# The second norm of x from three sums gathered in the down product, with the update of x split between VectorE and GpSimd

## The chip, the cores and the metric

The kernel runs on one core of a Trainium2 chip. The core has five engines with queues of their own: TensorE (matmul), VectorE, ScalarE, GpSimd and SyncE (which here only issues DMAs). They meet only through semaphores. The metric is the device time of one execution in microseconds.

## The reference, cut to what matters

Two transformer blocks follow one another on x of 512 positions by 1024 channels, all in float32. The change lies where the first block ends and the second begins:

```
# end of the first block
f = (silu(h @ w_gate) * (h @ w_up)) @ w_down
x = x + rms_norm(f, norm_ffn_post_g)
# start of the second block
h = rms_norm_2(x, norm1_g) * (1 + sc1) + sh1
proj = h @ w_in_2          # the linear attention's and the dilated attention's inputs
# rms_norm(v, g) = v * rsqrt(mean(v * v) + 1e-6) * g, the mean over the 1024 channels
```

The root of the second norm needs the mean square of the new x, which is the old x plus f times its own root and gain. Written out, with r the first root, o = f times gain: sum(x_new^2) = sum(x^2) + 2 r sum(x o) + r^2 sum(o^2).

## The kernel before, in words

Everything is kept transposed: channels on the 128 partitions in 8 tiles, the 512 positions along the row. A weight tile (`raw`, 128x1024, three slots) is loaded by SyncE, rounded by ScalarE to fp32r (`split_hi`, L1079), and VectorE makes the rest `w_lo` (`split_lo`, L1549). A product is three fp32r matmuls for each of 8 channel tiles (hi x hi, hi x lo, lo x hi, L598), so a unit of one output tile has 24.

*Down* (`down`, L864 on TensorE, L1358 on ScalarE, L1906 on VectorE) makes the 8 tiles of f. Each takes three weight slots in the order 1, 0, 2, and lands in O0 or O1 by turns. When a tile is done, ScalarE squares it into `sq` (L1305) and copies it into `oT` (L1306), and VectorE adds the square to `sqacc` (L1565) and computes two pieces of the second block's modulation vector from `ada` (L1883). Behind the last tile TensorE sums over the partitions with a matrix of ones, in plain f32: first `sqacc` (L612), then the square of the last tile (L614), both into S0.

*The first root and the update.* ScalarE makes the root with a logarithm and an exponential (`inverse_rms`, L1090 and L1091). VectorE (`post_norm`, L1587) then goes through the 8 tiles of x: `hbuf` = oT x gain x root (L1598), x = x + hbuf (L1606). ScalarE squares each new tile (L1083) and TensorE adds it to S0 (`sum_squares_by_tile`, L616). Behind its eight tiles VectorE splits the weights in slot 2 and clears `gacc` (L1943), which raises `m2_free`.

*The second root and h.* `inverse_rms` again; then, tile by tile, VectorE multiplies x with the root (L1579), ScalarE scales and shifts (L1097) and rounds to `h_hi` (L1098), VectorE takes the remainder `h_lo` (L1574). TensorE takes up each tile as it comes, for two units at once (`two_units`, L633): one gives the gate input `glr`, the other the first query tile.

*What follows.* ScalarE copies `glr` (L1389), splits slot 1 and goes on in a fixed order. TensorE multiplies `glr` with `wgate` (L893), then runs units with the level products of the linear attention (L923) between them. VectorE makes cumulative sums and seven masks before it raises the signal for the first level products.

The order on every engine is that of the code; nothing is scheduled at run time. Three queues matter here. SyncE waits for `m2_free` before it loads `wgate`, and all later weight tiles stand behind that in its queue. GpSimd issues the loads of `ada` and then waits for `m2_free` too, to number rows and columns for the masks. `h_hi` and `oT` are the same memory.

Of the kernel before, what the change touches and what calls it, by code (L numbers as in the profile page):

```python
# [26 lines left out]
P = 128  # L27
S = 512
# [150 lines left out]
def build(nc, a, out):  # L179
    with ExitStack() as ctx:  # L180
# [57 lines left out]
        (oT,), _ = region(h_at, ("oT", [KD, S], F32))  # L238
# [120 lines left out]
        x_sq_r = signal("x_sq_r")  # L359
        f_f32 = signal("f_f32", credit=1)  # L360
# [81 lines left out]
        def _(pool):  # L442
# [138 lines left out]
        def _(pe):  # L581
# [33 lines left out]

            def sum_squares_by_tile():  # L616

                for k in range(KD):
                    pe.wait_ge(sq_g[k % 2], w.next(sq_g[k % 2]))
                    pe.matmul(S0[:, :], ones[:, :], sq[:, k % 2, :], start=(k == 0),  # L620
                              stop=(k == KD - 1)).then_inc(sq_used[k % 2] if k < KD - 1 else ms_ready, 1)
                for g in range(2):
                    w.skip(sq_used[g], 4)
# [240 lines left out]
            def down(read):  # L864
                pe.wait_ge(f_ready, w.next(f_ready, times=NF - 1))

                def pair(late=None):
# [8 lines left out]
                with w.repeat(3, {**{split_ready[s]: 2 for s in range(3)}, (read[0], 1): 1, (read[1], 1): 1}):  # L876
                    pair()

# [5 lines left out]
            down(drained)  # L884
            sum_squares()


            sum_squares_by_tile()
# [177 lines left out]
        def _(act):  # L1066
# [245 lines left out]

            two = {**{raw_in[s]: 1 for s in range(2)}, **{(unit_done[s], 1): 1 for s in range(2)}}
# [11 lines left out]

            def new_x_squares():
                for k in range(KD):
                    act.wait_ge(x_ready, w.next(x_ready))
                    square(k, xT[:, k, :])
# [28 lines left out]
            def down(each):  # L1358
                split_hi(2, K=6)
                per = {**{raw_in[s]: 2 for s in range(3)}, **{(unit_done[s], 1): 2 for s in range(3)}, unit_done[2]: 2,  # L1360
                       (sq_used[0], 1): 1, (sq_used[1], 1): 1}
# [168 lines left out]
        def _(dve):  # L1530
            w = Waits(dve)
            for free in (*sq_used, f_f32, conv_gd, conv_vd, *drained_x, *ada_used, gate_read, up_read,
                         f_ready, *split_ready, gy_ready):
                dve.sem_inc(free, 1)
# [32 lines left out]

            def modulated_lo():

                dve.wait_ge(rstd_ready, w.next(rstd_ready))  # L1570

                def lo(k):
                    dve.wait_ge(n_hi, w.next(n_hi))
                    dve.tensor_tensor(h_lo[:, k, :], hbuf[:, k % 2, :], h_hi[:, k, :].bitcast(F32),  # L1574
                                      ALU.subtract).then_inc(h_ready, 1)

                for k in range(KD):
                    dve.wait_ge(h_ready, w.next(h_ready, ahead=2))
                    dve.tensor_tensor(hbuf[:, k % 2, :], xT[:, k, :], rstd[:, :], ALU.mult).then_inc(xr_ready, 1)  # L1579
                    if k >= 1:  # L1580
                        lo(k - 1)
                lo(KD - 1)
# [4 lines left out]
            def post_norm(from_, gain, then_scaled=None):  # L1587
# [14 lines left out]
                for k in range(KD):  # L1602
# [4 lines left out]
                    if then_scaled and k >= 1:  # L1607
                        lo(k - 1)
                if then_scaled:
                    lo(KD - 1)  # L1610
                    w.skip(h_ready, KD, ahead=2)
                else:
                    skip_squares()

# [312 lines left out]

            def square_and_modulation(g, c):

                add_squares(g)  # L1930
                modulation(c + 2 * NF - 2, g)

            down(square_and_modulation, {**sums, ada_in[0]: 2, ada_in[1]: 2, ada_used[0]: 2, ada_used[1]: 2}, skip_last_square, follows=True,
                 seventh=lambda g, c: add_squares(g))
# [6 lines left out]
            post_norm(oT, lambda k: col("norm_ffn_post_g", k))  # L1941
# [4 lines left out]
            modulated_lo()  # L1946
# [287 lines left out]
```

## Time and profile before

| | us |
|---|---|
| median of 3 runs (lowest, highest) | 1440.65 (1437.36, 1441.19) |
| the profiled execution | 1441.32 |
| its span, first to last instruction | 1439.3 |
| TensorE busy | 1390.4 (97%) |
| VectorE busy | 882.9 (61%) |
| ScalarE busy | 590.0 (41%) |
| GpSimd busy | 70.5 (5%) |
| TensorE's share of the chain that ended last | 90% |

Times in the text are microseconds from the start of the span of the profiled execution. PE is TensorE, PEld its weight loads, DVE VectorE, ACT ScalarE, POOL GpSimd and SP SyncE; L with a number is a line of the kernel. TensorE's busy share is no measure of its speed, since its clock has two levels (1.2 and 2.4 GHz) and a matmul is called busy at either. A row's time in brackets says how long the engine was idle before it, and what ended that. Down ends near 767.6, and the linear attention's first product starts near 788.6.

### The profile page before, as it was taken

The numbers are of one execution on the slowest core, as the hardware profiler recorded it, in microseconds if no ns is written. First come the engines' busy times: TensorE is split into PE (matmuls) and PEld (weight loads), VectorE is DVE, ScalarE is ACT, GpSimd is POOL, SyncE is SP. The second block draws the span as 40 slices with busy tenths as digits, with TensorE's granted clock in tenths as the row PEclk, the third lists the DMA queues.
The fourth block names the chain that finished last, engine by engine and source line by source line (L and its number), as shares of the span: only waits on it lengthen the run. The fifth ranks groups of instructions, "written<-read, shape, count | busy, mean of one in ns | idle before, by whom it ended". The sixth has DMA issues, their size and how long they took to land.

```text
span 1439.3 us, 18374 instructions
## 1 busy us (share of the span) xinstructions
PE 1390.4 (97%) x6330; PEld 1098.6 (76%) x6330; DVE 882.9 (61%) x1450; ACT 590.0 (41%) x966; POOL 70.5 (5%) x128
## 2 busy tenths in 40 slices
PE   7999999999999999999997999899989999999999
PEld 5777777767768888888884788677668888888887
DVE  5666677777567777774336688666556656655222
ACT  5455445543352323323224524466445444444221
POOL 4000000000001221211000000000000000000000
PEclk9999999999999999999998999999999999999999
DMA  5222212213216565565431122021112232223332
GB/s 186 100 73 74 74 59 78 77 54 114 99 44 201 187 196 192 187 195 160 136 109 59 44 74 74 30 74 59 55 60 77 97 102 87 102 96 107 103 95 84
DMA packets 42319, 146.72 MB, mean 102 GB/s; under 512 B 5392, under 2 KB 5664, under 8 KB 42272
## 3 DMA queue, kind: packets, MB, share of 16 engines
q1 hardware_dynamic: 34448, 120.39, 25.5%
q0 software_dynamic: 7824, 25.70, 5.4%
q8 instruction: 30, 0.49, 0.1%
q14 instruction: 17, 0.14, 0.0%
HBM read 143.97 MB, written 2.10 MB: 101 GB/s over the span
## 4 chain that ended last, share of the span: by engine, by line
PE 90%; DVE 5%; ACT 2%; issue 1%; DMA 0%; DVEq 0%; ACTq 0%
PE bank L598 62%; PE bank L713 12%; PE bank L670 3%; PE bank L633 3%; PE bank L735 2%; PE bank L754 1%; PE bank L923 1%; PE bank L772 1%; ACT w_hi L1079 1%; PE bank L620 1%; DVE w_lo L1549 1%; PE bank L639 1%; DVE gate_last L1739 0%; DVE gate_a L1739 0%; PE bank L775 0%
## 5 line engine op out<-in xcount | busy, mean ns | idle before, releaser
L1549 DVE TENSOR_TENSOR w_lo<-raw,w_hi 128x1024 fp32r<-128x1024 f32 (+1 forms) x225 | 272.2, 1212 | 176.1 <-ACT w_hi L1079 175.3
L1079 ACT ACTIVATE w_hi<-raw 128x1024 fp32r<-128x1024 f32 (+1 forms) x225 | 233.6, 1039 | 302.8 <-PE bank L598 282.0
L598 PE MATMUL bank<-h_hi,w_hi 128*128 128x512 f32 x872 | 346.3, 397 | 0.8 <-DVE gyf L2045 0.8
L598 PE MATMUL bank<-h_hi,w_lo 128*128 128x512 f32 x872 | 340.6, 391 | 0.0
L598 PE MATMUL bank<-h_lo,w_hi 128*128 128x512 f32 x872 | 340.5, 391 | 0.0
L598 PEld LDWEIGHTS bank<-h_hi,w_hi 128*128 128x128 f32 x872 | 164.2, 188 | 42.5 <-issue 7.7
L598 PEld LDWEIGHTS bank<-h_hi,w_lo 128*128 128x128 f32 x872 | 164.3, 188 | 34.6
L598 PEld LDWEIGHTS bank<-h_lo,w_hi 128*128 128x128 f32 x872 | 164.4, 188 | 34.2 <-issue 1.2
L598 PE MATMUL bank<-f_hi,w_lo 128*128 128x512 f32 x352 | 136.9, 389 | 0.0
L598 PE MATMUL bank<-f_hi,w_hi 128*128 128x512 f32 x352 | 136.9, 389 | 0.0
L598 PE MATMUL bank<-f_lo,w_hi 128*128 128x512 f32 x352 | 136.9, 389 | 0.0
L713 PE MATMUL bank<-h_hi,w_hi 128*128 128x512 f32 x240 | 98.4, 410 | 0.4 <-DVE ma L1745 0.4
L713 PE MATMUL bank<-h_hi,w_lo 128*128 128x512 f32 x240 | 93.9, 391 | 0.0
L713 PE MATMUL bank<-h_lo,w_hi 128*128 128x512 f32 x240 | 93.6, 390 | 0.0
L598 PEld LDWEIGHTS bank<-f_hi,w_hi 128*128 128x128 f32 x352 | 66.1, 188 | 13.8
L598 PEld LDWEIGHTS bank<-f_lo,w_hi 128*128 128x128 f32 x352 | 66.1, 188 | 13.7
L598 PEld LDWEIGHTS bank<-f_hi,w_lo 128*128 128x128 f32 x352 | 66.1, 188 | 13.7
L1883 DVE CUSTOM_DVE_ANT_0 ada<-ada,cond 128x512 f32<-128x512 f32 x96 | 63.7, 689 | 14.0 <-DMA ada<-in_w_ada 12.7
L483 POOL DMA_DIRECT2D ada<-in_w_ada x96 | 51.6, 538 | 350.9 <-DVE ada_sum L1883 344.7
L713 PEld LDWEIGHTS bank<-h_hi,w_hi 128*128 128x128 f32 x240 | 45.0, 188 | 21.4 <-issue 13.6
L1869 DVE TENSOR_TENSOR f_lo<-fbuf,f_hi 128x512 f32 (+1 forms) x44 | 30.5, 692 | 43.9 <-ACT f_hi L1517 22.0
L713 PEld LDWEIGHTS bank<-h_hi,w_lo 128*128 128x128 f32 x240 | 45.1, 188 | 10.1
(299 smaller groups left out, 1867.7 us busy)
## 6 DMA issues: line engine op xcount, KB each, us to landing
raw<-in_w_up SPq DMA_DIRECT2D x66, 512.0 KB, 3.2
raw<-in_w_mix SPq DMA_DIRECT2D x48, 512.0 KB, 3.2
ada<-in_w_ada POOLq DMA_DIRECT2D x96, 256.0 KB, 3.2
raw<-in_w_down SPq DMA_DIRECT2D x32, 512.0 KB, 3.5
raw<-in_w_in SPq DMA_DIRECT2D x25, 512.0 KB, 3.3
raw<-in_w_gate SPq DMA_DIRECT2D x22, 512.0 KB, 3.3
raw<-in_w_out SPq DMA_DIRECT2D x16, 512.0 KB, 3.3
raw<-in_w_down SPq DMA_DIRECT2D x16, 384.0 KB, 3.3
```

Source lines behind the costliest of these rows:

```text
L483: pool.dma_start(ada[:, half, :], a["w_ada"][bass.ds(t, 1), :, half * S:half * S + S] .rearrange("t p k -> (t p) k")).then_inc(ada_in[half ...
L598: last = pe.matmul(to[:, :], wt[:, slot, k, :], act_[:, rhs0 + k, :], start=(k == first and n == 0), stop=(k == K - 1 and n == 2))
L620: pe.matmul(S0[:, :], ones[:, :], sq[:, k % 2, :], start=(k == 0), stop=(k == KD - 1)).then_inc(sq_used[k % 2] if k < KD - 1 else ms_ready, 1)
L633: last = pe.matmul(to[g][:, :], wt[:, slot, k, :], act_[:, k, :], start=(k == 0 and n == 0), stop=(k == KU - 1 and n == 2))
L639: last = pe.matmul(S0[:, :], ones[:, :], x_sq[:, k, :], start=(k == 0), stop=(k == KU - 1))
L670: last = pe.matmul(banks[r][:, :], xt[:, k, P * r:P * r + P], wt[:, slot, 4 * kk:4 * kk + 4, :].rearrange("p a b -> p (a b)"), start=(k == ...
L713: last = pe.matmul(G[u % 2][:, :], wt[:, slot, k, :], act_[:, kr, :], start=(kr == 0 and m == 0), stop=(kr == length - 1 and m == 2))
L735: ins = pe.matmul(SB_[m][:, at_:at_ + n], qk_[h, i % 2, 0, P * r:P * r + P], qk_[h, i % 2, 1, 0:n], start=True, stop=True)
L1079: act.activation(w_hi[:, s, 0:K, :], raw[:, s, 0:K, :], ACT.Copy).then_inc(hi_ready[s], 1)
L1549: dve.tensor_tensor(w_lo[:, s, 0:K, :], raw[:, s, 0:K, :], w_hi[:, s, 0:K, :].bitcast(F32), ALU.subtract).then_inc(split_ready[s], 1)
L1869: dve.tensor_tensor(at_k(f_lo, j), fbuf[:, :], at_k(f_hi, j).bitcast(F32), ALU.subtract).then_inc(f_ready, 1)
L1883: dve.tensor_tensor_reduce(ada[:, half, :], ada[:, half, :], cond[:, half * S:half * S + S], 1.0, 0.0, ALU.mult, ALU.add, ada_sum[:, parit ...
```

## The change

The squares of the new x are no longer taken. Instead, three sums are gathered while down runs. ScalarE writes f times gain to `oT` (in place of f) and its square to `gained_sq`, besides the square of f itself; VectorE adds x times `oT` and `gained_sq` to the two halves of `cross_sum`. In the last tile of down, ahead of the slot 2 products, TensorE starts the sums of `sqacc`, and of both halves of `cross_sum` (`sums_so_far`); behind that tile it adds the last tile's share to each (`last_sums`). The sum of squares of the old x is still in S0 from the feed-forward's norm.

VectorE then puts the new mean square together in four instructions, ScalarE makes its root, and VectorE scales `oT` with the first root, two tiles at a time. GpSimd adds such a pair to x (`x_moved`), and VectorE multiplies the pair with the second root and takes the remainders as before. The eight steps of `post_norm` in this place, the eight squares and the eight sums by tile are gone. The split of slot 2 and the clearing of `gacc` stand in the code as before behind the update of x; since the update and the making of h are now one loop, they stand behind both.

```diff
+            for j in range(4):
+                pool.wait_ge(o_scaled, j + 1)
+                pool.tensor_tensor(xT[:, 2 * j:2 * j + 2, :], xT[:, 2 * j:2 * j + 2, :], oT[:, 2 * j:2 * j + 2, :],
+                                   ALU.add).then_inc(x_moved, 1)
...
+            def sums_so_far():
+
+                w.skip(sq_g[0], 4)
+                w.skip(sq_used[1], 4)
+                pe.wait_ge(sq_used[0], w.next(sq_used[0], times=4))
+                pe.matmul(S1[:, :], ones[:, :], sqacc[:, :], start=True, stop=False)
+                pe.wait_ge(gained_used[0], 5)
+                pe.wait_ge(gained_used[1], 4)
+                for m in range(2):
+                    pe.matmul(TB[m][:, :], ones[:, :], cross_sum[:, m, :], start=True, stop=False)
+
+            def last_sums():
+
+                pe.wait_ge(sq_g[1], w.next(sq_g[1], times=4))
+                pe.matmul(S1[:, :], ones[:, :], sq[:, 1, :], start=False, stop=True).then_inc(ms_ready, 1)
+                pe.wait_ge(gained_sq_r[1], 4)
+                pe.matmul(T1[:, :], ones[:, :], gained_sq[:, 1, :], start=False, stop=True)
+                pe.wait_ge(cross_r, 1)
+                pe.matmul(T0[:, :], ones[:, :], cross[:, 1, :], start=False, stop=True).then_inc(cross_ms, 1)
...
                         unit(OB[g], 0, f_hi, f_lo, K=NF, first=-1)
+                        if g and sums:
+                            sums()
...
-            down(drained)
-            sum_squares()
-
-
-            sum_squares_by_tile()
+            down(drained, sums_so_far)
+            last_sums()
...
+            def gained_tile(g, c):
+
+                gain = col("norm_ffn_post_g", c)
+                act.wait_ge(gained_used[g], w.next(gained_used[g], ahead=1))
+                act.wait_ge(sq_used[g], w.next(sq_used[g], ahead=1))
+                act.activation(sq[:, g, :], OB[g][:, :], ACT.Square).then_inc(sq_g[g], 1)
+                act.activation(oT[:, bass.ds(c, 1), :].rearrange("p a s -> p (a s)"), OB[g][:, :], ACT.Identity,
+                               scale=gain).then_inc(gained[g], 1)
+                act.activation(gained_sq[:, g, :], OB[g][:, :], ACT.Square, scale=gain).then_inc(gained_sq_r[g], 1)
+                act.wait_ge(gained_sq_r[g], w.next(gained_sq_r[g]))
+                act.sem_inc(drained[g], 1)
...
-            down(lambda g, c: out_tile(g, c, oT, OB))
-            inverse_rms()
+            down(gained_tile, {(gained_used[0], 1): 1, (gained_used[1], 1): 1, gained_sq_r[0]: 1, gained_sq_r[1]: 1})
+            inverse_rms(sums=S1)
             split_hi(2)
-            new_x_squares()
-
-
-            inverse_rms()
+            act.wait_ge(ms2_ready, 1)
+            then(act.activation(sqacc[:, :], sqacc[:, :], ACT.Ln, scale=1.0 / D, bias=eps6[:, :]))
+            act.activation(sqacc[:, :], sqacc[:, :], ACT.Exp, scale=-0.5).then_inc(rstd2_ready, 1)
             modulated_hi(lambda k: mod_a[:, 0, k:k + 1], lambda k: modc[:, k:k + 1])
...
+            def modulated(k, root):
+
+                dve.wait_ge(h_ready, w.next(h_ready, ahead=2))
+                dve.tensor_tensor(hbuf[:, k % 2, :], xT[:, k, :], root[:, :], ALU.mult).then_inc(xr_ready, 1)
+
+            def remainder(k):
+
+                dve.wait_ge(n_hi, w.next(n_hi))
+                dve.tensor_tensor(h_lo[:, k, :], hbuf[:, k % 2, :], h_hi[:, k, :].bitcast(F32),
+                                  ALU.subtract).then_inc(h_ready, 1)
...
+            def modulated_with_update():
+
+                def scaled(j):
+                    pair = slice(2 * j, 2 * j + 2)
+                    dve.tensor_tensor(oT[:, pair, :], oT[:, pair, :], rstd[:, :].rearrange("p (a s) -> p a s", a=1)
+                                      .broadcast_to([P, 2, S]), ALU.mult).then_inc(o_scaled, 1)
+
+                dve.wait_ge(rstd_ready, w.next(rstd_ready))
+                dve.wait_ge(cross_ms, 1)
+                then(dve.tensor_tensor(sqacc[:, :], T1[:, :], rstd[:, :], ALU.mult))
+                then(dve.scalar_tensor_tensor(out=sqacc[:, :], in0=T0[:, :], scalar=2.0, in1=sqacc[:, :], op0=ALU.mult,
+                                              op1=ALU.add))
+                then(dve.tensor_tensor(sqacc[:, :], sqacc[:, :], rstd[:, :], ALU.mult))
+                dve.tensor_tensor(sqacc[:, :], sqacc[:, :], S0[:, :], ALU.add).then_inc(ms2_ready, 1)
+                scaled(0)
+                scaled(1)
+                dve.wait_ge(rstd2_ready, 1)
+                dve.wait_ge(x_moved, 1)
+                modulated(0, sqacc)
+                modulated(1, sqacc)
+                for j in range(1, 4):
+                    if j < 3:
+                        scaled(j + 1)
+                    remainder(2 * j - 2)
+                    dve.wait_ge(x_moved, j + 1)
+                    modulated(2 * j, sqacc)
+                    remainder(2 * j - 1)
+                    modulated(2 * j + 1, sqacc)
+                remainder(KD - 2)
+                remainder(KD - 1)
...
+            then(dve.memset(cross_sum[:, :, :], 0.0))
+
+            def add_cross(g, c):
+
+                dve.wait_ge(gained[g], w.next(gained[g]))
+                then(dve.tensor_tensor(cross[:, g, :], at_k(xT, c), at_k(oT, c), ALU.mult))
+                then(dve.tensor_tensor(cross_sum[:, 0, :], cross_sum[:, 0, :], cross[:, g, :], ALU.add))
+                dve.wait_ge(gained_sq_r[g], w.next(gained_sq_r[g]))
+                dve.tensor_tensor(cross_sum[:, 1, :], cross_sum[:, 1, :], gained_sq[:, g, :], ALU.add).then_inc(gained_used[g], 1)
+
+            def last_cross():
+
+                skip_last_square()
+                dve.wait_ge(gained[1], w.next(gained[1]))
+                dve.tensor_tensor(cross[:, 1, :], xT[:, 7, :], oT[:, 7, :], ALU.mult).then_inc(cross_r, 1)
...
-            post_norm(oT, lambda k: col("norm_ffn_post_g", k))
+            modulated_with_update()
             split_lo(2)
             dve.memset(gacc[:, :, :], 0.0).then_inc(m2_free, 1)
 
 
-            modulated_lo()
```

The pieces of the modulation vector are still computed in down, ahead of the splits as before. How the rows move on VectorE, from the last tile of down to the units of the linear attention, before the change (`hbuf` scratch, `mod_a` the modulation's gain):

```order
L1940 TENSOR_TENSOR mod_a<-mod_a,cols 128x8
L1598 SCALAR_TENSOR_TENSOR hbuf<-oT,cols,rstd 128x512 x2
L1606 TENSOR_TENSOR xT<-xT,hbuf 128x512
...
L1606 TENSOR_TENSOR xT<-xT,hbuf 128x512 x2
L1549 TENSOR_TENSOR w_lo<-raw,w_hi 128x1024
L1943 MEMSET gacc 128x2048
L1579 TENSOR_TENSOR hbuf<-xT,rstd 128x512 x2
L1574 TENSOR_TENSOR h_lo<-hbuf,h_hi 128x512
L1579 TENSOR_TENSOR hbuf<-xT,rstd 128x512
L1574 TENSOR_TENSOR h_lo<-hbuf,h_hi 128x512
```

The `gacc` clearing is the instruction right before the first multiplication of the new x with its root. In the same place with the change:

```order
L1632 TENSOR_TENSOR sqacc<-sqacc,bank 128x512
L1623 TENSOR_TENSOR oT<-oT,rstd 128x1024 x2
L1602 TENSOR_TENSOR hbuf<-xT,sqacc 128x512 x2
L1623 TENSOR_TENSOR oT<-oT,rstd 128x1024
L1607 TENSOR_TENSOR h_lo<-hbuf,h_hi 128x512
L1602 TENSOR_TENSOR hbuf<-xT,sqacc 128x512
L1607 TENSOR_TENSOR h_lo<-hbuf,h_hi 128x512
...
L1602 TENSOR_TENSOR hbuf<-xT,sqacc 128x512
L1607 TENSOR_TENSOR h_lo<-hbuf,h_hi 128x512 x2
L1580 TENSOR_TENSOR w_lo<-raw,w_hi 128x1024
L2028 MEMSET gacc 128x2048
```

The multiplications with the root (`hbuf<-xT`) now stand between the scalings of `oT`, and the slot 2 split and the `gacc` clearing have moved from ahead of the first of them to behind the last remainder.

GpSimd's queue behind the loads of `ada`, before and then with the change:

```order
L483 DMA ada<-in_w_ada 128x512
L165 REGISTER_ALU
L165 COMPARE_AND_BRANCH
L487 IOTA mj 128x128
L488 IOTA mi 128x128
```

The two rows behind the loop of loads number rows and columns. With the change:

```order
L490 DMA ada<-in_w_ada 128x512
L165 REGISTER_ALU
L165 COMPARE_AND_BRANCH
L495 TENSOR_TENSOR xT<-xT,oT 128x1024 x4
L499 IOTA mj 128x128
L500 IOTA mi 128x128
```

GpSimd had nothing but row and column numbers there, and now has four adds of 128x1024 ahead of them. SyncE's queue at the same place, with what each transfer waits for, is the same before and after but for line numbers:

```order
L499 DMA raw<-in_w_in 128x1024 [waits split_ready2]
L560 DMA wgate<-in_gla_w_gate 16x256 [waits m2_free]
L499 DMA raw<-in_w_in 128x1024 [waits split_ready1]
L499 DMA raw<-in_w_in 128x1024 [waits split_ready0]
L499 DMA raw<-in_w_in 128x1024 [waits split_ready2]
```

The load of the gate weights waits for the `gacc` clearing, and the further tiles of `w_in` wait behind it in the queue.

## Rows read from the trace of the kernel before

**Rows 1.** The chain that ended last, 740 to 800: start us, us, work.

```profile
767.62 0.86 PE bank L612 x2
768.49 0.96 PE bank L614 x2
...
771.00 1.41 DVE hbuf L1598 x2
...
773.73 10.35 PE bank L620 x16
...
785.56 0.70 DVE hbuf L1579
...
788.63 11.42 PE bank L633 x40
```

**Rows 2.** Busy by stretch: stretch, us, PE busy (records), clock; last row all engines.

```profile
776.00:780.00 4.00, 4.00 (x6) 0.57 0.00 0
...
788.00:790.00 2.00, 1.37 (x3) 0.50 0.99 395
...
820.00:830.00 10.00, 9.08 (x60) 7.60 (x59) 9.07 (x28) 3.96 (x5) 0.00 (x0) 1.00 0.10 28
```

**Rows 3.** Timeline of PE at the resumption: start, us, what.

```profile
790.05 0.63 PE L633 MATMUL bank<-h_hi,w_hi 128*128 128x512 f32 x1
790.48 0.63 PE L633 MATMUL bank<-h_lo,w_hi 128*128 128x512 f32 x1
```

**Rows 4.** Busy in down's last stretch: PE, PEld, DVE, ACT, POOL, clock.

```profile
740.00:765.00 25.00, 25.00 (x112) 20.68 (x111) 7.21 (x10) 6.06 (x7) 0.00 (x0) 1.00 0.24 79
```

**Rows 5.** Groups by line on DVE, 340 to 800: count | busy, mean ns.

```profile
L1549 DVE TENSOR_TENSOR w_lo<-raw,w_hi 128x1024 fp32r<-128x1024 f32 x70 | 85.6, 1222 | 65.8 <-ACT w_hi L1079 65.7
...
L1579 DVE TENSOR_TENSOR hbuf<-xT,rstd 128x512 f32<-128x512 f32 x8 | 5.4, 691 | 0.5 <-ACT rstd L1091 0.3
```

**Rows 6.** Timeline between down and the linear attention, ACT, DVE and SP.

```profile
767.66 0.60 ACT L1305 ACTIVATE sq<-bank 128x512 f32<-128x512 f32 x1 [2.97 <-PE bank L598]
...
783.46 1.76 DVE L1943 MEMSET gacc<- 128x2048 f32 x1 [0.38 <-issue]
...
785.25 0.34 SPq L560 DMA_DIRECT2D wgate<-in_gla_w_gate  x1
...
785.64 1.37 SPq L499 DMA_DIRECT2D raw<-in_w_in  x3
...
798.06 0.69 DVE L1574 TENSOR_TENSOR h_lo<-hbuf,h_hi 128x512 fp32r<-128x512 f32 x1 [0.69 <-ACT h_hi L1098]
```

**Rows 7.** Timeline of POOL and DVE at the program's start.

```profile
13.05 1.28 POOL L463 TENSOR_TENSOR sqacc<-sqacc,sq 128x512 f32<-128x512 f32 x1
...
15.78 1.77 POOL L463 TENSOR_TENSOR sqacc<-sqacc,sq 128x512 f32<-128x512 f32 x1
16.31 1.79 DVE L1619 SCALAR_TENSOR_TENSOR y_lo<-xT,cols,y_hi 128x512 fp32r<-128x512 f32 x1
...
19.35 2.31 DVE L1549 TENSOR_TENSOR w_lo<-raw,w_hi 128x1024 fp32r<-128x1024 f32 x1
20.66 2.15 POOL L463 TENSOR_TENSOR sqacc<-sqacc,sq 128x512 f32<-128x512 f32 x1
```

**Rows 8.** DMA issues, 784 to 812: count, KB each, us to landing.

```profile
raw<-in_w_in SPq DMA_DIRECT2D x5, 512.0 KB, 3.5
wgate<-in_gla_w_gate SPq DMA_DIRECT2D x1, 16.0 KB, 1.7
```

**Rows 9.** Timeline behind the stage: the slot 1 split, and the last mask.

```profile
801.72 1.04 ACT L1079 ACTIVATE w_hi<-raw 128x1024 fp32r<-128x1024 f32 x1
...
826.38 0.23 DVE L1970 TENSOR_SCALAR masks<-mx 128x128 int32<-128x128 f32 x1
```

**Rows 10.** The chain that ended last, 780 to 900.

```profile
826.74 2.82 PE bank L923 x32
829.56 5.67 PE bank L598 x24
```

More of the change, by code:

```diff
@@ L237, in build @@
         h_lo = sb("h_lo", [KD, S], F32R)
-        (oT,), _ = region(h_at, ("oT", [KD, S], F32))
+        (oT, cross, cross_sum, gained_sq), h_end = region(
+            h_at, ("oT", [KD, S], F32), ("cross", [2, S], F32), ("cross_sum", [2, S], F32), ("gained_sq", [2, S], F32))
+        assert h_end <= h_at + 2 * KD * S * 4
         tmp_at = base[0]
@@ L614, in sum_squares @@
                 pe.matmul(S0[:, :], ones[:, :], sq[:, 1, :], start=False, stop=True).then_inc(ms_ready, 1)
[L616 to L623, printed above, removed]
             def two_units(to, slots, squares=False):
@@ L862, in ffn, with down, pair @@
                     unit(G0, 0, h_hi, h_lo)
-            def down(read):
+            def sums_so_far():
[14 more added lines that the diff above has]
+                pe.matmul(T0[:, :], ones[:, :], cross[:, 1, :], start=False, stop=True).then_inc(cross_ms, 1)
+            def down(read, sums=None):
                 pe.wait_ge(f_ready, w.next(f_ready, times=NF - 1))
-                def pair(late=None):
+                def pair(late=None, sums=None):
                     for g in range(2):
@@ L875, in down @@
                 pair(f_ready)
-                with w.repeat(3, {**{split_ready[s]: 2 for s in range(3)}, (read[0], 1): 1, (read[1], 1): 1}):
+                with w.repeat(2, {**{split_ready[s]: 2 for s in range(3)}, (read[0], 1): 1, (read[1], 1): 1}):
                     pair()
+                pair(sums=sums)
             for g in range(2):
@@ L1324, in _ @@
             out_tile(1, 7, oT_mix, G)
[L1326 to L1329, printed above, removed]
             inverse_rms()
@@ L1356, in _, with down @@
             w.start(unit_done, "down")
-            def down(each):
+            def down(each, more):
                 split_hi(2, K=6)
                 per = {**{raw_in[s]: 2 for s in range(3)}, **{(unit_done[s], 1): 2 for s in range(3)}, unit_done[2]: 2,
-                       (sq_used[0], 1): 1, (sq_used[1], 1): 1}
+                       (sq_used[0], 1): 1, (sq_used[1], 1): 1, **more}
                 with w.repeat(3, per) as c:
@@ L1568, in modulated_lo @@
             def modulated_lo():
                 dve.wait_ge(rstd_ready, w.next(rstd_ready))
[L1572 to L1575, printed above, removed]
                 for k in range(KD):
-                    dve.wait_ge(h_ready, w.next(h_ready, ahead=2))
-                    dve.tensor_tensor(hbuf[:, k % 2, :], xT[:, k, :], rstd[:, :], ALU.mult).then_inc(xr_ready, 1)
+                    modulated(k, rstd)
@@ L1580, in modulated_lo @@
                     if k >= 1:
-                        lo(k - 1)
-                lo(KD - 1)
+                        remainder(k - 1)
+                remainder(KD - 1)
[26 more added lines that the diff above has]
+                remainder(KD - 2)
+                remainder(KD - 1)
@@ L1606, in post_norm @@
                     dve.tensor_tensor(xT[:, k, :], xT[:, k, :], hbuf[:, k % 2, :], ALU.add).then_inc(x_ready, 1)
-                    if then_scaled and k >= 1:
+                    if k >= 1:
                         lo(k - 1)
[L1609 to L1613, printed above, removed]
+                lo(KD - 1)
+                w.skip(h_ready, KD, ahead=2)
             def scaled_lo(k):
@@ L1926, in _, with seventh @@
             split_lo(2, K=6)
+            then(dve.memset(cross_sum[:, :, :], 0.0))
[9 more added lines that the diff above has]
+                dve.tensor_tensor(cross[:, 1, :], xT[:, 7, :], oT[:, 7, :], ALU.mult).then_inc(cross_r, 1)
             def square_and_modulation(g, c):
                 add_squares(g)
+                add_cross(g, c)
                 modulation(c + 2 * NF - 2, g)
-            down(square_and_modulation, {**sums, ada_in[0]: 2, ada_in[1]: 2, ada_used[0]: 2, ada_used[1]: 2}, skip_last_square, follows=True,
-                 seventh=lambda g, c: add_squares(g))
+            def seventh(g, c):
+                add_squares(g)
+                add_cross(g, c)
+            down(square_and_modulation, {**sums, ada_in[0]: 2, ada_in[1]: 2, ada_used[0]: 2, ada_used[1]: 2, gained[0]: 1, gained[1]: 1,
+                                         gained_sq_r[0]: 1, gained_sq_r[1]: 1, dve_step: 4}, last_cross, follows=True,
+                 seventh=seventh)
             for parity in range(2):
```

9 lines of the change are left out of this document (7 added, 2 removed).

## Prediction

> **What bounds the kernel now.** I read the chain that ended last first. Between 767.6 and 788.6 us it leaves the weight products: the sums of squares of the down product end at 769.45, ScalarE makes a root, VectorE updates x in eight steps of two instructions while ScalarE squares the new tiles and TensorE sums them (10.35 us), ScalarE makes the second root, one tile goes through VectorE, ScalarE and VectorE again, and TensorE resumes at 788.63 [rows 1]. So 21 us lie between the last product of down and the first of the linear attention. TensorE's clock falls twice in them: it is granted 0.57 of full speed in 776 to 780, and after 4.5 us without work it resumes at 0.50, its 1.2 GHz level [rows 2], with 0.43 us from one matmul to the next [rows 3]; a unit of 24 takes 5.67 us, 0.24 each, at 2.4 GHz [rows 10].
>
> Next I read who waits behind the stage. ScalarE splits the next weight tile at 801.72, and from there its queue, VectorE's cumulative sums and its mask instructions follow one another without a hole in the chain of waits until 826.6 [rows 9]; TensorE runs out of work before that (0.9 us idle between 820 and 830, [rows 2]) and takes up the level products at 826.74 [rows 10]. What sets the time past this stage is thus the split at 801.72, not only TensorE's start at 788.63. The tile for it (slot 1) was loaded at 785.64, behind the gate weights at 785.25, which wait for the memset of gacc that ends at 783.46 + 1.76 = 785.22 [rows 6].
>
> **The change, step by step** (all in the clock of the profiled execution).
> *In down.* TensorE gets three plain f32 products inside the last tile where it had one behind it. One is 0.86 us [rows 1], so the last product ends at 767.62 + 3 x 0.86 = 770.2. Each tile also has one more ScalarE pass and three more VectorE instructions of about 0.7 [rows 5]; both engines are under a third busy in 740 to 765, where VectorE works 7.21 and ScalarE 6.06 us of 25 [rows 4], and what they split is needed a unit later: nothing. If that cover were gone, each tile would cost up to 3 us. The clearing of cross_sum stands behind the slot 2 split and costs nothing either.
> *The three sums.* The square of the last tile starts 0.05 behind 770.2; before, 1.79 us lay from its start (767.66, [rows 6]) to the end of the sum at 769.45, and VectorE had the root 1.55 later. Now: sum at 772.05, root at 773.6. The other two products follow the sum (2 x 0.86), the last at 773.85. Four dependent VectorE instructions of 0.7 and a little between them: 2.95, until 776.8. The second root, 1.5 as before (784.08 to 785.56, [rows 1]), is out at 778.3, hidden by the two scalings of x's update.
> *The update.* A scaling of two tiles is a 128x1024 tensor_tensor, 1.22 us; that and the add on GpSimd replace two of the four old 0.7 instructions per pair. GpSimd's add of two tiles is not in this trace. Its 128x512 add takes 1.28 us alone [rows 7]. Upper bound: twice that, 2.56; lower: times VectorE's own ratio 1222/691 [rows 5], 2.26. I take 2.4, between the near ends.
> *The two engines together.* This is the step that decides. GpSimd's add that starts at 15.78 takes 1.77 instead of 1.28, VectorE's scalar_tensor_tensor that starts at 16.31 takes 1.79, where two of them take 1.41 elsewhere [rows 1]; its split at 19.35 takes 2.31 for 1.22, the add at 20.66 then 2.15 [rows 7]. Each is longer by about what the other still had to run: 16.31 + 1.79 = 18.10, which is 0.55 behind the end of the add at 15.78 + 1.77 = 17.55, most of one instruction. They run one after the other, in turn. All VectorE instructions of the new loop read two SBUF tensors, as those did.
> The Trainium skill has this as a rule (SBUF — State Buffer, "SBUF: two separate sides"): the port pair that VectorE and GpSimd share is an exclusive lock, held for a whole instruction by a VectorE instruction with two SBUF inputs or a GpSimd one that reads SBUF; the trace agrees, with its 1.79 for 0.7. Its GPSIMD Engine Reference (3.1, Elementwise) gives 4497 ns for 2048 elements; between that and 1.28 for 512 an estimate for 1024 is 2.35, which would move the sum below by -0.1. By the rule every add of the new loop costs VectorE its full 2.4; the other reading of the same rows, a rate that both share, would cost it less where it has gaps anyway, and is rival (2).
>
> Run in turn from 776.8: scaling 0 to 778.0, scaling 1 to 779.2, add 0 to 781.65, add 1 to 784.1 (or after the first two tiles; the next line is the same), tile 0 and 1 multiplied to 785.5, scaling 2 to 786.7, remainder 0 at 787.4. Add 2 to 789.8; two multiplications, a remainder, scaling 3 and a remainder to 793.8; add 3 to 796.2. Then the rest: multiplication 4, remainder 3, multiplication 5 to 798.3, and from there VectorE waits for ScalarE's two passes, some 1.5 per tile (what 788.63 - 785.56 leaves beside two instructions of 0.7, [rows 1]); the last remainder ends at 803.5, where it ended at 798.06 + 0.69 = 798.75 before [rows 6]. So TensorE starts at 787.5, 1.1 earlier than now, but is fed slowly: it ends at 805.0, or 810.6 if its clock stays at 1.2 GHz (48 matmuls, 0.43 each), against 801.9.
>
> *What is late next.* The slot 2 split and the gacc memset stood ahead of the tile loop and now stand behind it on VectorE, and the memset's signal holds SyncE's queue: the gate weights, and behind them every further weight tile. 803.5 + 1.2 + 1.75 = 806.4; the load goes out 0.42 later as before [rows 6] and lands 3.5 us after that [rows 8], at 810.3. ScalarE's split of slot 1, ahead of all its other work, starts at 810.35 instead of 801.72: **+8.6**. Either end of TensorE (805.0 or 810.6) is hidden by or equal to it. TensorE waits at the gate product until 808.2 (wgate lands 1.7 after its issue, [rows 8]), then does in 24 to 25 us what took it from 801.9 to about 826 before, until about 832.5, and waits for the masks until 826.74 + 8.6 = 835.4, so nothing of the 8.6 is absorbed.
> *Clock.* That last wait of some 3 us may put TensorE at 1.2 GHz again. It costs nothing if the clock holds; if it falls, each matmul takes 0.43 for 0.24, and a stretch of 4 to 7 us costs 2 to 3. I take 1, nearer to nothing since the wait is shorter than the one at 784.
>
> Sum: 8.6 + 1 = +9.6. The profiled execution took 1441.32 with a span of 1439.3 (2.0 lie around it); it becomes 1450.9. The median of the runs is 0.67 below it: **1450.3**.
>
> **Rivals.**
> (1) *No turn-taking to speak of* for these forms. For: the rows are few, adds of half the size at the start of the program. Against: three collisions there, all alike [rows 7]. Then the same order run side by side gives remainder 0 at 783.8, remainder 7 at 795.1, the memset at 798.1, the tile landed at 802.0 against 801.72: +0.3, so 1441; TensorE's start 4.7 earlier is worth nothing since ScalarE waits for the load.
> (2) *Partly in turn* (the adds slip into gaps of VectorE, or the lock is let go within an add). Half the effect: +4 to +5, 1445.
> (3) *The whole earlier start arrives*: TensorE begins 4.7 us sooner (783.9) and the end follows, 1436. That needs the memset's signal by 801.72 - 4.7 - 3.9 = 793.1; beyond that point every us of lateness is a us lost. The unhindered order reaches 798.1, so for it both the adds and VectorE's loop would have to be a third quicker than any row.
> (4) *Both clock losses land*: TensorE stays at 1.2 GHz through the two units (810.6, 0.3 behind the load) and again behind the masks, 8.9 + 3: 1452.6.
>
> **How the numbers follow.** Forecast in its own form 0.72, (1) 0.09, (2) 0.08, (3) 0.03, (4) 0.08. The unknown add (2.26 to 2.56) moves it by -0.6 to +0.5, the clock by -1 to +2; with (2) half in and (4) in, the range is 1445 to 1454. This kernel can tell a change from 0.3%, 4.3 us. Case (3) alone is faster by more than that: 0.03; same is (1) and a small part of (2): 0.11; slower 0.86.
>
> **What the new profile would show.** Three f32 products within the last tile; the four new VectorE instructions from about 774 to 777; GpSimd's four adds, alone 2.3 to 2.6 us, some recorded up to 3.6, and VectorE instructions of 0.69 beside them recorded at 2 to 3 us; the first attention matmul near 787.5; the gacc memset near 804.7; ScalarE waiting for the raw tile by DMA until about 810; TensorE idle ahead of wgate's product and ahead of the first level products. I am wrong if VectorE's loop shows 0.69 beside the adds, or if the memset ends before 798, or if ScalarE does not wait for the load.

## The result, and the profile after

| | before | after |
|---|---|---|
| median of 5 runs on one chip (lowest, highest), us | 1441.19 (1437.36, 1442.43) | 1449.87 (1448.71, 1450.22) |
| span of the profiled execution, us | 1439.3 | 1448.1 |
| TensorE busy, us | 1390.4 | 1388.0 |
| VectorE busy, us | 882.9 | 901.2 |
| GpSimd busy, us | 70.5 | 81.4 |

The changed kernel takes 1.0058 of the time of before, 95% interval 1.0047 to 1.007: 8.4 us slower (6.8 to 10.1). The forecast was 1450.3. All ratios here compare fast runs; the one slow run, of 3582.41 us among the twelve of e2_vector_adds, is in that kernel's median of 1446.54 (1446.19 without it) and not in its ratio.

One thing must be taken out before rows are compared. ScalarE's square of down's last-but-one tile starts at 754.03 in this trace and at 752.69 in the one of before. These 1.34 us are not the change's doing: the square of down's first tile is already 1.41 late (664.42 against 663.01), the six steps from there to the last-but-one tile take 89.61 against 89.68, and e7_before_late_signal below, which up to there has the code of before, has the same lag (754.06). Where I call a time "own", I have subtracted it.

The chain of waits of after, cut from 760 to 840: start us, us, work. It answers to [rows 1] and [rows 10].

```profile
779.51 1.13 DVE oT L1623
780.64 2.29 issue
782.93 3.36 DVE hbuf L1602 x2
786.29 1.14 DVE oT L1623
787.43 0.61 DVE h_lo L1607
788.13 2.67 DVE hbuf L1602
...
802.61 0.69 DVE h_lo L1607
803.31 1.14 DVE w_lo L1580
804.44 0.38 issue
804.82 1.78 DVE gacc L2028
806.61 0.34 SPq L572
807.00 3.42 DMA raw<-in_w_in
...
835.15 0.24 DVE masks L2054
835.51 2.82 PE bank L948 x32
```

TensorE is not in it between 779.5 and 835.5. VectorE's loop leads into the slot 2 split and the memset, the memset into SyncE's queue, the load into ScalarE's split, and from there the same queue of splits, cumulative sums and masks as before ends at the level products: 835.51 where it was 826.74, so 8.77 later, 7.43 own.

The two engines of the update, timeline of after: start us, us, engine and line, what, how often, idle before.

```profile
778.29 2.35 DVE L1623 TENSOR_TENSOR oT<-oT,rstd 128x1024 f32<-128x1024 f32 x2
782.93 3.36 DVE L1602 TENSOR_TENSOR hbuf<-xT,sqacc 128x512 f32<-128x512 f32 x2 [2.29 <-issue]
...
788.13 2.67 DVE L1602 TENSOR_TENSOR hbuf<-xT,sqacc 128x512 f32<-128x512 f32 x1
...
793.97 2.69 DVE L1602 TENSOR_TENSOR hbuf<-xT,sqacc 128x512 f32<-128x512 f32 x1
```

```profile
779.60 5.54 POOL L495 TENSOR_TENSOR xT<-xT,oT 128x1024 f32<-128x1024 f32 x2 [49.22 <-DVE oT L1623]
787.51 2.75 POOL L495 TENSOR_TENSOR xT<-xT,oT 128x1024 f32<-128x1024 f32 x1 [2.37 <-DVE oT L1623]
793.35 2.76 POOL L495 TENSOR_TENSOR xT<-xT,oT 128x1024 f32<-128x1024 f32 x1 [3.09 <-DVE oT L1623]
```

A record's length includes the wait for the other engine. The scalings end at 780.64 and the two adds at 785.14: 4.50 between, 2.25 for one add. The two multiplications, woken by the first add, end 1.15 behind the second one (786.29), which is about what they take alone. At 788.03 VectorE ends a remainder; 788.03 + 2.25 is 790.28, where the add recorded at 787.51 ends (790.26); the multiplication recorded at 788.13 ends at 790.80. An instruction of 0.69 is recorded at 2.67, because it stands behind nearly a whole add.

The load that decides, on ScalarE, then TensorE at the gate product and at the first level products, answering to [rows 9] and [rows 2]:

```profile
810.44 1.06 ACT L1104 ACTIVATE w_hi<-raw 128x1024 fp32r<-128x1024 f32 x1 [5.47 <-DMA raw<-in_w_in]
```

```profile
808.32 3.75 PE L918 MATMUL bank<-glr,wgate 16*128 16x512 f32 x4 [3.28 <-DMA wgate<-in_gla_w_gate]
...
835.04 0.39 PE L610 MATMUL bank<-h_hi,w_lo 128*128 128x512 f32 x1
835.51 1.71 PE L948 MATMUL bank<-gq,gk 64*128 64x128 f32 x19
```

The windows of after (stretch, length, busy of PE, PEld, DVE, ACT, POOL, then the granted clock):

```profile
776.00:780.00 4.00, 0.00 (x0) 0.00 (x0) 3.90 (x6) 1.35 (x2) 0.40 (x1) 0.68 0.00 0
780.00:784.00 4.00, 0.00 (x0) 0.00 (x0) 1.71 (x2) 0.00 (x0) 4.00 (x2) 0.50 0.00 0
...
810.00:814.00 4.00, 4.00 (x8) 1.95 (x7) 1.23 (x1) 3.56 (x5) 0.00 (x0) 0.50 0.65 250
814.00:820.00 6.00, 6.00 (x26) 4.94 (x25) 1.23 (x1) 5.84 (x11) 0.00 (x0) 0.92 0.49 171
834.00:838.00 4.00, 3.92 (x38) 3.34 (x37) 3.68 (x9) 1.65 (x2) 0.00 (x0) 1.00 0.03 8
```

ScalarE waited 5.47 us for the load. Before, nothing waited for it: the tile was issued at 785.64, landed 3.5 later, near 789.1, and was split at 801.72, right behind ScalarE's copy of `glr`:

```profile
801.22 0.59 ACT L1389 ACTIVATE glr<-bank 16x512 f32<-16x512 f32 x1 [3.19 <-PE bank L633]
```

So the load had about 12.6 us of slack before. From the end of the memset to the split it takes 3.86 in after (806.58 to 810.44); the memset of before could have ended as late as 797.86 (801.72 - 3.86) instead of 785.22. In after it ends at 806.58, own 805.24, which is 7.4 beyond that: the 7.4 of the stage.

TensorE waited 3.28 us for `wgate`, came back at 1.2 GHz (0.50) and therefore reached the level products only just in time for the masks: no wait there, and the clock stayed at 1.00.

### The profile page after: what moved, and what is told of

It is laid out like the page before. It is cut to its first block and busy times, and to the rows that moved or that the text cites. A ratio compares the mean times of both kernels' runs of the same rounds, so it can differ in the third digit from the quotient of the medians.

```text
span 1448.1 us, 18405 instructions
## 1 busy us (share of the span) xinstructions
PE 1388.0 (96%) x6322; PEld 1097.1 (76%) x6322; DVE 901.2 (62%) x1465; ACT 591.1 (41%) x966; POOL 81.4 (6%) x132
## 5 line engine op out<-in xcount | busy, mean ns | idle before, releaser
L1945 DVE CUSTOM_DVE_ANT_0 ada<-ada,cond 128x512 f32<-128x512 f32 x96 | 63.7, 688 | 14.5 <-DMA ada<-in_w_ada 14.1
```

The costliest lines, as they stand in the source:

```text
L1945: dve.tensor_tensor_reduce(ada[:, half, :], ada[:, half, :], cond[:, half * S:half * S + S], 1.0, 0.0, ALU.mult, ALU.add, ada_sum[:, parit ...
```

## The experiments

My theory had two independent parts: the signal that hands the weight buffer back is late (`m2_free` behind the whole loop), and GpSimd's adds and VectorE's instructions go in turn. The rivals were that the load's lateness is hidden (the slack takes it up), that the turns cost nothing, and that something else in the new loop (its length, its waits for ScalarE) is the cost.

Besides the time I read one distance in each trace: from the square of down's last-but-one tile to the first level product, 74.05 us in before (752.69 to 826.74). What lies ahead of it or far behind it is not in it. All ratios are against before on the same chip; each kernel ran 5 to 12 times.

| | ratio [95%] | as us | distance against before |
|---|---|---|---|
| after | 1.0058 [1.0047, 1.007] | +8.4 | +7.43 |
| e1_signal_early | 1.0009 [1.0001, 1.0018] | +1.3 | +1.94 |
| e2_vector_adds | 1.0028 [1.0018, 1.0039] | +4.0 | +4.05 |
| e3_both | 0.9978 [0.9969, 0.9987] | -3.2 | -1.93 |
| e4_beside_adds | 1.0072 [1.0059, 1.0085] | +10.4 | +11.41 |
| e5_scale_first | 0.9979 [0.9967, 0.999] | -3.0 | -2.74 |
| e6_tile_adds | 1.0049 [1.0033, 1.0065] | +7.1 | +7.60 |
| e7_before_late_signal | 1.0028 [1.0017, 1.004] | +4.0 | +4.04 |
| e8_masks_early | 0.997 [0.9957, 0.9983] | -4.3 | -3.74 |

**e1_signal_early.** The changed kernel with the buffer handed back as soon as the sums are there; the slot 2 split and the memset stay where they are.

```
                 dve.wait_ge(cross_ms, 1)
+                dve.sem_inc(m2_free, 1)
...
-            dve.memset(gacc[:, :, :], 0.0).then_inc(m2_free, 1)
+            dve.memset(gacc[:, :, :], 0.0)
```

> The changed kernel, but the signal that frees SyncE's queue (m2_free) is raised on VectorE as soon as both sums are there, and no longer by the gacc memset behind the loop. Theory (the lateness reaches the end through the load behind that signal): the load goes out near 776 instead of 807, ScalarE splits slot 1 right behind the gate input's copy, near 804.9 instead of 810.44, and wgate's product starts near 805; 1449.9 - 5.6 = 1444.3 us. VectorE's loop stays as it is, last remainder at 803.3. Rival (TensorE's slow feeding in the loop is the whole loss, and the load is only late beside it): no change, 1449.9.

Measured 1443.18 us where 1444.3 was expected; 5.6 was to come back, and in the distance it is 5.5. SyncE's queue, then ScalarE, in its timelines:

```profile
775.65 0.34 SPq L572 DMA_DIRECT2D wgate<-in_gla_w_gate  x1
```

```profile
804.60 0.59 ACT L1420 ACTIVATE glr<-bank 16x512 f32<-16x512 f32 x1 [1.81 <-PE bank L636]
805.10 1.04 ACT L1104 ACTIVATE w_hi<-raw 128x1024 fp32r<-128x1024 f32 x1
```

The load now goes out 30 us earlier, the split follows ScalarE's copy of `glr` without a wait, and 5.5 of the 7.4 us are gone from the distance (7 of 8.4 in time). GpSimd's adds are as long as in after (5.54 for the first two), so the turns are not what this edit touched. What is left, +1.9, comes through `glr`: VectorE's last remainder is late, so TensorE ends its two units late, and ScalarE's copy of `glr` stands ahead of the split. The copy starts at 804.60, less the 1.43 us by which this trace lags that of before 803.17: 1.95 later than the 801.22 of before.

**e7_before_late_signal.** The same part alone, the other way round: before, with the split and the memset moved behind `modulated_lo`.

```
             post_norm(oT, lambda k: col("norm_ffn_post_g", k))
+            modulated_lo()
             split_lo(2)
...
-            modulated_lo()
```

> The kernel before with one part of the change alone: the split of the carried lower half and the zeroing of the accumulator, which hands the weight buffer back, stand behind the split of the modulated input instead of ahead of it. Norm, scaling and additions are as before. Theory (the load behind that signal sets the start of the next weights): VectorE reaches the zeroing near 800, it ends near 801.7, the first load lands about 3.9 us later, near 805.6, and ScalarE's split of the first slot, at 801.72 before, starts there: +3.9 us, 1445 to 1446. Rival (the load has slack, what follows waits for TensorE's own work): no change, 1441 to 1442.

Measured 1446.08 against 1442.05, +4.04 in the distance; 3.9 was worked out. Its timelines of VectorE and ScalarE:

```profile
801.62 1.76 DVE L1944 MEMSET gacc<- 128x2048 f32 x1 [0.38 <-issue]
```

```profile
807.08 1.06 ACT L1079 ACTIVATE w_hi<-raw 128x1024 fp32r<-128x1024 f32 x1 [4.42 <-DMA raw<-in_w_in]
```

That settles the first part: without any of the new norm, a signal that comes too late makes the whole stage late. It does not cost all of its lateness. The memset ends at 803.38, less the lag of 1.37 us 802.01, and so 16.8 later than before; the first 12.6 are the load's slack, and the 4.2 beyond 797.86 are what the distance shows (4.04). The other late signals follow the same count, each less its trace's lag: the memset is 3.8 beyond in e2 and 7.4 in e6, and the split is 4.0 and 7.6 later than before.

**e2_vector_adds.** The changed kernel with the adds on VectorE, the late signal kept.

```
-            for j in range(4):
-                pool.wait_ge(o_scaled, j + 1)
-                pool.tensor_tensor(xT[:, 2 * j:2 * j + 2, :], xT[:, 2 * j:2 * j + 2, :], oT[:, 2 * j:2 * j + 2, :],
-                                   ALU.add).then_inc(x_moved, 1)
...
+                def moved(j):
+                    pair = slice(2 * j, 2 * j + 2)
+                    dve.wait_ge(o_scaled, j + 1)
+                    dve.tensor_tensor(xT[:, pair, :], xT[:, pair, :], oT[:, pair, :], ALU.add).then_inc(x_moved, 1)
```

`moved(0)` stands behind the second scaling, `moved(j)` ahead of the multiplications of pair j.

> The changed kernel, but VectorE adds the scaled pair to x itself, 128x1024 as GpSimd did; the late signal stays. VectorE gets four more instructions of 1.22. Theory (the two engines take turns, a GpSimd add of 2.25 costs VectorE as much): the loop gets shorter in spite of that, last remainder near 799.3 instead of 803.3, the load and everything behind it 4.0 earlier, 1445.9 us. Rival (GpSimd's adds run beside VectorE and cost only their own latency): VectorE's four adds come on top of its work, the last remainder at 803.3 or later, 1449.9 to 1453.

Measured 1446.54 where 1445.9 was expected. Timeline of VectorE:

```profile
782.99 1.29 DVE L1597 TENSOR_TENSOR hbuf<-xT,sqacc 128x512 f32<-128x512 f32 x2 [0.46 <-issue]
...
785.94 1.22 DVE L1624 TENSOR_TENSOR xT<-xT,oT 128x1024 f32<-128x1024 f32 x1
```

VectorE has four more instructions of 1.22 us, and still its last remainder ends 28.2 us behind down's last square (800.52 - 772.34), where in after it is 31.7 (803.30 - 771.59): 3.5 shorter, 4.0 was expected. Help from GpSimd cost more than it took over.

**e4_beside_adds.** e2, with GpSimd doing adds of the same size that nobody waits for, on other data. The output of them is not used.

```
+            both = cond[:, :].rearrange("p (a s) -> p a s", a=2)
+            for j in range(4):
+                pool.wait_ge(o_scaled, j + 1)
+                then(pool.tensor_tensor(gvt[:, 0:2, :], both, both, ALU.add))
```

> As the one in which VectorE adds the pairs itself, and GpSimd makes four more 128x1024 adds of a constant tile into unused memory, one after each scaling; nobody waits for them, so they cost VectorE only what sharing costs. Theory (turns, whole instructions): 4 x 2.2 less the gaps that VectorE has anyway; the last remainder near 807 to 808, 1454 to 1455 us. Rival (no turns): as without them, 1445.9. Partly in turn: about 1450.

Measured 1451.97. Timelines of VectorE and GpSimd:

```profile
780.59 2.92 DVE L1629 TENSOR_TENSOR xT<-xT,oT 128x1024 f32<-128x1024 f32 x1
...
788.07 2.91 DVE L1629 TENSOR_TENSOR xT<-xT,oT 128x1024 f32<-128x1024 f32 x1
...
800.49 1.22 DVE L1629 TENSOR_TENSOR xT<-xT,oT 128x1024 f32<-128x1024 f32 x1
```

```profile
787.69 2.21 POOL L496 TENSOR_TENSOR gvt<-cond 128x1024 f32<-128x1024 f32 x1 [2.43 <-DVE oT L1623]
794.32 2.21 POOL L496 TENSOR_TENSOR gvt<-cond 128x1024 f32<-128x1024 f32 x1 [4.42 <-DVE oT L1623]
```

Work that no instruction depends on makes the distance 7.4 us longer than in e2. The same VectorE add is 1.22 where GpSimd is idle and 2.91 beside an add of 2.21. That shows the turns apart from every data dependence.

Not all of the 7.4 is turns. The last remainder ends at 806.04, which behind down's last square is 6.2 later than in e2: 1.56 for each add of 2.2, since part of an add falls where VectorE has a gap anyway. The rest arises behind the split of slot 1, where TensorE, slow from its wait for `wgate`, keeps ScalarE waiting for a query tile:

```profile
814.00:820.00 6.00, 6.00 (x13) 4.13 (x13) 2.45 (x2) 5.90 (x10) 0.00 (x0) 0.50 0.62 206
```

```profile
823.17 0.60 ACT L1436 ACTIVATE gq<-bank 128x512 f32<-128x512 f32 x1 [1.18 <-PE bank L610]
```

Less the lag of 1.37 the split is 10.06 later than before and the first level product 11.41, so 1.35 come in between. In after the clock is back to 0.92 in 814 to 820, ScalarE does not wait there, and the split and the level product are late by the same amount. My figure (1454 to 1455) was too high by 2 to 3: I had let each add cost its 2.2 less the gaps, and took the gaps too small.

**e6_tile_adds.** The changed kernel with GpSimd's adds cut in halves.

```
-            for j in range(4):
-                pool.wait_ge(o_scaled, j + 1)
-                pool.tensor_tensor(xT[:, 2 * j:2 * j + 2, :], xT[:, 2 * j:2 * j + 2, :], oT[:, 2 * j:2 * j + 2, :],
-                                   ALU.add).then_inc(x_moved, 1)
+            for k in range(8):
+                pool.wait_ge(o_scaled, k // 2 + 1)
+                pool.tensor_tensor(xT[:, k, :], xT[:, k, :], oT[:, k, :], ALU.add).then_inc(x_moved, 1)
...
```

VectorE's waits for `x_moved` are changed to match: one ahead of each multiplication, for its own tile.

> The changed kernel in which GpSimd adds single 128x512 tiles (eight additions) in place of pairs (four of 128x1024); the late signal stays. Theory (the two engines take turns by whole instructions): a scaling or a product of VectorE waits for at most one short addition (about 1.3 us instead of 2.25), so the first product of the stage stands about 2 us earlier than in the changed kernel (TensorE starts it near 786 instead of 788.2); GpSimd's additions sum to about 10 us as before. The load behind the late signal is still late by nearly as much, so the time is 1448.5 to 1450. Rival (each engine gives way within an instruction): VectorE's mean lengths beside the additions stay as they are, TensorE starts at 788, and the time stays 1449.9.

Measured 1448.81. Timelines of VectorE and GpSimd:

```profile
784.32 2.29 DVE L1622 TENSOR_TENSOR oT<-oT,rstd 128x1024 f32<-128x1024 f32 x1
...
788.81 1.76 DVE L1606 TENSOR_TENSOR h_lo<-hbuf,h_hi 128x512 fp32r<-128x512 f32 x1
```

```profile
778.79 6.74 POOL L495 TENSOR_TENSOR xT<-xT,oT 128x512 f32<-128x512 f32 x4 [49.22 <-DVE oT L1622]
786.69 3.34 POOL L495 TENSOR_TENSOR xT<-xT,oT 128x512 f32<-128x512 f32 x2 [1.16 <-DVE oT L1622]
```

Half right. The records beside an add shrink from 2.67 to 1.6 to 1.8, as turns by whole instructions want, and ScalarE gets its first product 12.0 us behind down's last square instead of 14.1. But TensorE starts 16.59 behind that square in both kernels: the third scaling, which stands ahead of the first remainder, now waits for an add too (2.29 for 1.22). I had followed the first product only and not what stands behind it. The adds sum to 13.4 us, not 10: each one meets a VectorE instruction. Smaller pieces gain nothing.

**e3_both, e5_scale_first, e8_masks_early.** e3 has the edits of e1 and e2. e5 is e3 with `scaled(0)` moved ahead of `dve.wait_ge(cross_ms, 1)` and `moved(0)` ahead of `scaled(1)`; `m2_free` is raised ahead of that `scaled(0)`. e8 is e5 with the mask instructions moved ahead of the split of the fourth unit:

```
-            for n in (2, 3, 4):
+            for n in (2, 3):
                 split_lo(gla_slot(n))
+            dve.wait_ge(const_ready, w.next(const_ready, times=2))
+            then(dve.tensor_tensor(masks[:, 0, :], mi[:, :], mj[:, :], ALU.bitwise_xor))
...
+            split_lo(gla_slot(4))
```

> Both edits together. Theory: last remainder near 799.3, gate input copied near 800.4, slot 1 split at 800.9 instead of 810.44: 1449.9 - 9.5 = 1440.4 us, within noise of the kernel before (0.9994 of it). If the two causes were one and the same (removing either is enough), it would be no faster than the better of the two alone, some 1444 to 1446.

> The kernel with both edits (buffer handed back early, pair additions on VectorE), in which VectorE now scales the first pair of tiles as soon as the first root stands, ahead of the mean square of the gained activations, and adds that pair before it scales the next. Theory (the chain of VectorE from the root to the first product bounds the stage): one instruction of about 0.69 us leaves the way to the second root's cross sum only where VectorE idled for the root, so the last remainder ends about 0.5 us earlier than in that kernel and the time falls by about 0.5, from 1438.7 to 1438.2. Rival (the scaling delays the mean square by its whole length and TensorE and ScalarE wait for that): 0.7 later, 1439.4. Rival (TensorE's product of the stage bounds it, not VectorE): no change, 1438.7.

> The kernel with both edits and the early scaling, in which VectorE also computes the masks of the linear attention before the split of the fourth unit and the cumulative sums, in a stretch where it waited for ScalarE. Theory (TensorE's 0.94 us of idleness before the first products of the levels waits for these masks): that wait goes, and the time is about 0.9 below that kernel's, near 1437.3. Rival (the masks stand behind another input that comes last there, or push the split of the fourth unit back by as much): no change, near 1438.2.

Measured 1438.73, 1439.01 and 1436.9. TensorE at the first level products, in the timelines of e3, then e8:

```profile
827.52 1.71 PE L943 MATMUL bank<-gq,gk 64*128 64x128 f32 x19 [0.94 <-DVEq L2100]
```

```profile
823.58 1.60 PE L943 MATMUL bank<-gq,gk 64*128 64x128 f32 x17
```

With both costs taken away the new norm is a gain: e3 is faster than before, by 1.9 us in the distance; the 3.2 in time hold something from outside it. The early signal alone is not what gains on before, as far as the traces tell (no run raises it early in before): there the load had its 12.6 us of slack, and the split waited for the copy of `glr`. In e3 that copy comes 1.95 earlier:

```profile
801.98 0.59 ACT L1415 ACTIVATE glr<-bank 16x512 f32<-16x512 f32 x1 [1.80 <-PE bank L631]
```

(801.98 less the lag of 2.71 is 799.27, against 801.22.) The two parts add up without overlap worth naming: in the distance e1 gives back 5.5 and e2 3.4, together 8.9, and e3 9.4, where 9.5 was expected. e5 is 0.8 shorter in the distance, in the direction expected, though the 0.5 was worked out with 0.69 us for the scaling, which takes 1.22. Its time shows no difference from e3; by time alone it is unclear. Its profile runs the stretch between the two attentions, shown at the end, at 0.76 and 0.56 where e3's runs at 1.00, which in that execution is enough to hide 0.8 us. e8 removes TensorE's wait of 0.9 us for the masks and is 1.0 shorter than e5 in the distance; by the ratios the difference (0.9979 to 0.997) is within their intervals. It is the fastest kernel of the study, 0.997 of before and clear of 1.

## Why the prediction was right

*In down.* Right. The last tile takes 17.56 us from square to square (754.03 to 771.59) where it took 14.97: +2.59, three products of 0.86. The additional work of VectorE and ScalarE per tile cost nothing: 89.61 us for six tiles against 89.68.

*The three sums.* Right to 0.2. VectorE ends its four instructions at 778.29, own 776.95; 776.8 was worked out.

*GpSimd's add.* 2.25 and, in e4, 2.21; I took 2.4. The lower bound, VectorE's own ratio times 1.28, was the right reading of the rows.

*In turn.* Right, and shown by e4: VectorE and GpSimd do not meet only through semaphores, as the first section has it. The Trainium skill's rule (SBUF — State Buffer, "SBUF: two separate sides"), a port pair held for a whole instruction, agrees with the records of 2.67 for 0.69 and 2.91 for 1.22; e6, with shorter adds and shorter waits, fits it too. Rival (1) is refuted by the same rows, and (3) by the load's wait. Rival (2) is refuted as it stands, by the records and by +8.4 for its +4 to +5; its first half, adds that slip into VectorE's gaps, is in e4 for 2.6 of 8.8 us.

*The end of the loop.* This term was too large. The last remainder ends at 803.30, own 801.96; 803.5 was worked out. Four adds were each 0.15 shorter than I took. The rest is VectorE's pace: I let an instruction of 0.69 take 0.7 and one of 1.22 take 1.2, but where one does not wait for the other the next begins 0.61 and 1.14 later (787.43 and 786.29 in the chain above). By the fourth add the two had made it 1.4 us early (796.11, own 794.77, worked out as 796.2).

*What is late next.* Right, and shown by e1 and e7. The split of slot 1 starts at 810.44 instead of 801.72: 8.72, of which 7.4 own, against 8.6; what is missing is the loop's end, own 1.5 us earlier than worked out. The prediction had the slack right: its rival (1) lets the memset end at 798.1 and charges 0.3 for it.

*Clock.* Wrong in its place, and so unpaid. I expected TensorE to wait some 3 us for the masks and come back slow. It came back slow already from the wait for `wgate`, 0.50 in 810 to 814, ran its units at 1.2 GHz while it would have waited anyway, and met the masks with no wait. By an estimate from these rows (4 us at 0.50, 6 at 0.92) it lost 2.5 us of full speed there. The low clock was paid out of idle time. The term of 1 is not in the trace, nor is rival (4): the two units end near 805.0, not 810.6; in e6, where TensorE did wait 1.77 us there, 834 to 838 shows 0.85. The term is not empty in general: in e4 the low clock behind the wait for `wgate` lasted to 820 and cost 1.35.

*The sum.* I had 8.6 + 1 = 9.6. The stage itself is 7.4 dearer. In the profiled pair 1.34 us ahead of the change make that 8.8; over all runs it is 8.4, with an interval of 6.8 to 10.1 that holds both 7.4 and 9.6. That the median was met to 0.4 us is in part luck: two terms were 1 us too large each (8.6 for 7.4, and 1 for nothing), something outside the stage took up about 1, and the median of before is 0.5 higher over five runs (1441.19) than over the three that the forecast started from (1440.65). The first-named cause and its order of size were right.

## What to carry to other kernels

Before a loop is made longer or two loops are merged, look at what stands behind them in the same queue: a signal that frees a buffer and moves from ahead of the loop to behind it costs nothing while the load behind it has slack (12.6 us here) and its whole further lateness after that. Work out the last harmless moment first: the time at which the tile is used, less the time from the signal to the tile's landing. One line that raises the signal earlier gives the loss back, up to the next thing that is late (5.5 of 7.4 us of the stage here). Work moved from VectorE to GpSimd is no help where both read SBUF at the same time; here the four adds were cheaper on the busy engine. When an edit makes an engine idle, check whether another term (a low clock, a later start) is paid out of that same idle time before adding both: in after it was, in e4 it was not.

## What was unexpected of the hardware

When GpSimd has a second add ready and VectorE is woken by the end of the first, GpSimd goes first: adds 0 and 1 run back to back (4.50 us behind the scalings), and the multiplication recorded at 782.93 waits for the second. Against that, with single adds between VectorE instructions, the two alternate. I had left open which it would be. In e4 it is the other way: VectorE's add, which needs no signal from GpSimd, already stood waiting when GpSimd's first add ended, and went in between the two (its record ends at 783.51, theirs at 785.26). That fits an order in which the instruction that is ready first goes first, but e4's adds also wait for each other by a semaphore, and no run separates the two.

Profiled executions differ in parts of the code that no edit touches. One is the start, 1.34 us as above. The other lies between the linear and the dilated attention, where TensorE waits for a norm. The windows of after, then of e3:

```profile
925.00:930.00 5.00, 2.25 (x8) 1.28 (x7) 2.60 (x7) 4.48 (x8) 0.00 (x0) 0.76 0.00 0
930.00:935.00 5.00, 5.00 (x14) 3.70 (x13) 5.00 (x6) 0.00 (x0) 0.00 (x0) 0.55 0.48 141
```

```profile
920.00:925.00 5.00, 4.22 (x18) 3.03 (x17) 4.14 (x5) 1.65 (x4) 0.00 (x0) 1.00 0.11 36
925.00:930.00 5.00, 3.72 (x21) 2.62 (x20) 3.84 (x5) 1.79 (x3) 0.00 (x0) 1.00 0.51 174
```

The profiled execution of after runs that piece at 0.76 and 0.55, e3 at 1.00 throughout (also 1.00 in 915 to 920 and 930 to 935). That of before falls there too, to 0.94, 0.50 and 0.88 in 915 to 930. The shortfalls of the clock, 5 x 0.24 + 5 x 0.45, are 3.4 us of full speed, which is as large as some of the differences in question. A difference of 1 or 2 us between two profiled spans is thus no evidence by itself, and this is why the distance over the stage stands beside every time above. What decides whether the clock falls there stays open.
